# Low halves of the projection weights made on GpSimd in two instructions instead of on VectorE in one

## What is computed

```python
h = _rmsnorm(x, pre_norm[l])
proj = h @ w_in[l]
(a_q, a_k, a_v, sb_q, sb_k, sb_v, f_q, f_k, f_v, f_logit, m_q, gate) = jnp.split(proj, COL_SPLITS, axis=-1)
o_a = _diff_attention(...)      # softmax of two maps, a = p[:, 0] - lam * p[:, 1], then a head norm
o_b = _stick_breaking(...)      # log_sigmoid(z) plus a reversed cumulative sum of log_sigmoid(-z)
o_c = _forgetting_attention(...)  # softmax with a cumulative forget term
o_m = _memory_attention(...)    # 256 memory keys
y = jnp.concatenate([o_a, o_b, o_c, o_m], axis=-1) * jax.nn.silu(gate)
x = x + _rmsnorm(y @ w_out[l], post_norm[l])
```

## Time and profile before

| | us |
|---|---|
| three timed runs | 2762.78, 2762.99, 2768.42 |
| median | 2762.99 |
| profiled execution, its own time | 2765.74 |
| span in its trace | 2763.5 |
| first block | 131 |
| second block | 2249 |
| third block and the change to it | 383.5 |
| PE busy in the second block | 2048.0 |

### The profile page before, as it was taken

The page is one execution under the profiler, slowest core; times in us unless marked ns, Lnnn a source line. Parts: engine busy times, 40 slices in busy tenths (PEclk is TensorE's granted clock), DMA queues, the critical chain, the costliest instruction groups (busy, mean ns, idle before and its releaser), DMA issues. The chain is left out here.

```text
span 2763.5 us, 73142 instructions
## 1 busy us (share of the span) xinstructions
PE 2458.7 (89%) x27422; PEld 1673.8 (61%) x27422; DVE 1814.8 (66%) x5009; ACT 1638.1 (59%) x4453; POOL 1139.3 (41%) x1808
## 2 busy tenths in 40 slices
PE   5589899999899999998989999989999997589998
PEld 4467566666766666666666666666666665334443
DVE  7547798776578887765699877657898765221111
ACT  5336675567667755676677556766775567321121
POOL 6313355456434454564254545642445456200000
PEclk9699999999999999999999999999999999689999
DMA  6235784479858843798598537985884379652331
GB/s 200 75 81 115 130 151 95 66 144 157 160 104 146 145 97 64 141 157 159 94 154 141 103 66 140 156 163 104 147 145 94 60 130 159 162 173 85 113 107 46
DMA packets 934554, 340.56 MB, mean 123 GB/s; under 512 B 766244, under 2 KB 925100, under 8 KB 934188
## 3 DMA queue, kind: packets, MB, share of 16 engines
q1 hardware_dynamic: 933752, 334.83, 61.9%
q0 software_dynamic: 448, 1.05, 0.1%
HBM read 80.83 MB, written 26.84 MB: 39 GB/s over the span
## 5 line engine op out<-in xcount | busy, mean ns | idle before, releaser
L1407 POOL TENSOR_TENSOR rows<-rows 128x512 f16<-128x512 f32 (+3 forms) x864 | 865.9, 1016 | 948.7 <-ACT rows L1365 945.1
L1211 PE MATMUL job<-wt,big 128*128 128x128 f16 x10752 | 680.4, 220 | 46.3 <-DVE gate_s L1497 16.7
L1211 PEld LDWEIGHTS job<-wt,big 128*128 128x128 f16 x10752 | 629.2, 99 | 112.9 <-DVE gate_s L1497 27.4
L1211 PE MATMUL job<-big,wt 128*128 128x512 f16 x2688 | 674.1, 383 | 10.1 <-PEq L672 5.2
L1365 ACT CAST rows<-rows 128x512 f16<-128x512 f32 (+3 forms) x864 | 463.3, 549 | 227.2 <-DVE rows L1489 115.5
L1272 PE MATMUL mixed<-values,rows 128*128 128x64 f16 (+1 forms) x8544 | 446.6, 202 | 107.1 <-DMA rows<-rows 78.3
L1272 PEld LDWEIGHTS mixed<-values,rows 128*128 128x128 f16 x8544 | 393.0, 100 | 235.0 <-DMA rows<-rows 112.2
L1377 ACT ACTIVATE rows<-rows,neg_max 128x512 f32<-128x512 f32 (+3 forms) x704 | 447.7, 638 | 72.7 <-DVE neg_max L1464 70.0
L1456 DVE TENSOR_SCALAR_CACHE_REDUCE rows<-scores 128x512 f32<-128x512 f32 (+3 forms) x704 | 399.6, 587 | 122.3 <-POOL rows L1407 92.9
L1257 PE MATMUL scores<-stack 128*128 128x512 f16 (+3 forms) x1600 | 432.8, 350 | 21.2 <-DVE rows L1456 14.8
L1211 PEld LDWEIGHTS job<-big,wt 128*128 128x128 f16 x2688 | 243.8, 99 | 248.7 <-issue 15.1
(11 more groups left out here) (142 smaller groups left out, 2558.0 us busy)
## 6 DMA issues: line engine op xcount, KB each, us to landing
stack<-planes SPq DMA_DIRECT2D x160, 192.0 KB
ws<-w_in SPq DMA_DIRECT2D x56, 512.0 KB, 4.7
y_halves<-y_out_halves SPq DMA_DIRECT2D x64, 256.0 KB, 2.9
rows<-y_halves SPq DMA_DIRECT2D x16, 1024.0 KB, 8.2
rows<-rows SPq DMA_TRANSPOSE x864, 3.3
rows<-x SPq DMA_DIRECT2D x16, 512.0 KB, 5.1
ws<-w_out SPq DMA_DIRECT2D x16, 512.0 KB, 3.7
stack<-x SPq DMA_DIRECT2D x16, 512.0 KB, 4.8
```

Of the source, the lines that this page charges most:

```text
L1211: last = nc.tensor.matmul(dst, lhs, rhs, start=(k0 == 0 and q == 0), stop=(k1 == KT and q == len(pairs) - 1))
L1407: nc.gpsimd.tensor_tensor(halves_of(tau, 1, w), scored(plan.chunk_at(g, m, k0), 0, w), halves_of(tau, 0, w), ALU.subtract).then_inc(low_po ...
```

## The change

The instruction at L1424 goes from DVE. POOL gets two in its place: a `tensor_scalar` that multiplies the strip by 64 in place in `ws`, and, after a wait for that (semaphore `w_wide`), a `tensor_tensor` that subtracts the high half and writes the low half. In the planner the task `widen` moves from DVE's table to POOL's, behind `lo`, and its length goes from 1.14 to 3.6. All five orders are planned anew with that. No other rank or length differs.

```diff
-    "dve": {"low": 3.02114, "weigh": 3.66090, "lo_dve": 5.58491, "widen": 5.68258, "post": 5.97032,
+    "dve": {"low": 3.02114, "weigh": 3.66090, "lo_dve": 5.58491, "post": 5.97032,
...
-    "pool": {"root": 0.00000, "lo": 1.00000},
+    "pool": {"root": 0.00000, "lo": 1.00000, "widen": 2.00000},
...
-            q["widen"].append((("w_lo", n), ("convert", (n, t, kind)), [("w_hi", n)], 1.14, 0.08))
+            q["widen"].append((("w_lo", n), ("convert", (n, t, kind)), [("w_hi", n)], 3.6, 0.1))
...
+                def convert(c):
+                    n, t, kind = c
+                    hi, lo = wt[:, kind, 0], wt[:, kind, 1]
+                    wide = ws[:, n % 2, :].rearrange("p (k n) -> p k n", k=KT)
+                    pool.wait_ge(w_hi, n + 1)
+                    nc.gpsimd.tensor_scalar(wide, wide, W_SCALE, None, ALU.mult).then_inc(w_wide, 1)
+                    pool.wait_ge(w_wide, n + 1)
+                    nc.gpsimd.tensor_tensor(lo, wide, hi, ALU.subtract).then_inc(w_ready, 1)
...
-                    dve.wait_ge(w_hi, n + 1)
-                    nc.vector.scalar_tensor_tensor(
-                        wt[:, kind, 1], ws[:, n % 2, :].rearrange("p (k n) -> p k n", k=KT), W_SCALE,
-                        wt[:, kind, 0], op0=ALU.mult, op1=ALU.subtract).then_inc(w_ready, 1)
```

More of the change, by code:

```diff
@@ L1022, in build @@
         w_in_sem = [sem(f"w_landed{b}") for b in range(2)]
-        w_hi, w_ready = sem("w_hi"), sem("w_ready")
+        w_hi, w_wide, w_ready = sem("w_hi"), sem("w_wide"), sem("w_ready")
         stacked = [sem(f"stacked{c}") for c in range(NC)]
@@ L1399, in inverse_root @@
                     nc.gpsimd.tensor_tensor(root[:, 3:4], y, rz[:, 0:1], ALU.mult).then_inc(root_step, 1)
+                def convert(c):
[6 more added lines that the diff above has]
+                    nc.gpsimd.tensor_tensor(lo, wide, hi, ALU.subtract).then_inc(w_ready, 1)
                 for op, *args in plan.orders["pool"]:
                     g = args[0]
+                    if op == "convert":
+                        convert(*args)
                     if op == "lo":
@@ L1419, in low @@
                         .then_inc(j_free, 1)
-                def convert(c):
-                    n, t, kind = c
-                    dve.wait_ge(w_hi, n + 1)
-                    nc.vector.scalar_tensor_tensor(
-                        wt[:, kind, 1], ws[:, n % 2, :].rearrange("p (k n) -> p k n", k=KT), W_SCALE,
-                        wt[:, kind, 0], op0=ALU.mult, op1=ALU.subtract).then_inc(w_ready, 1)
                 def stick_chunk(g, n, m, c, w):
@@ L1570, in _ @@
                     g = args[0] if args else None
-                    if op == "convert":
-                        convert(*args)
                     if op == "halves":
```

## The result

The changed kernel takes 2850.2 us (median of 4 runs, 2844.7 to 2857.7) against 2762.9 before. The measured ratio is 1.0325, with a 95% interval of 1.0304 to 1.0346 (the two medians alone give 1.0316, or 87 us). The forecast was 2774 with a range up to 2795. The direction was right and the size was not: +90 us by the ratio instead of +11. In what follows a ratio is turned into us with 2763, so 0.1% is 2.8 us. Rows and busy times are of one profiled execution each, so their differences carry a few us of scatter.

The account below looks back on a forecast made before the run. PE's fixed work plus its idle time was taken as the bound; 2765.7 + 25 - 12 - 8 + 6 = 2777 for the profiled execution, 2774 for the median (2763 + 11). Range 2750 to 2795, the forecast's own 2769 to 2781.

Parts of the forecast that it names:

- The bound: Second block: time is PE's fixed work plus its idle time, 201 us; POOL rises from 48 to some 56%.
- Removed, -12: DVE loses 55 conversions, mostly relieving stick and diff units, so PE waits less for banks: -12 us, bounds 0 and -33.
- Moves on PE, +25: Later strips and moved V and Q jobs give gate banks too little time, so PE idles: +25 us, bounds +10 and +30.
- Mixes later, -8: Stick units of lanes 1 to 3: more work between scores and mix shortens waits for landings: -8 us, bounds 0 and -20.
- Low halves behind the pair, +6: POOL's queue, memory, diff and forget units: low halves delayed, 0.2 us for each of 32 pairs, +6 us, bounds 0 and +60.
- SP and late weights at nothing: SP's strip loads start up to 2.1 us later with transposes behind them; the planned order covers that, cost zero.
- Rival 3: POOL: first instruction as costly as the second, pair 4.7 us, low halves late on an unprepared order; about 2797, chance 0.09.
- Rival 4: Diff units: DVE's two-input instructions blocked at the shared port by POOL pairs; 2774 + 14 = 2788, chance 0.05.
- Rival 1: Stick and diff units: DVE's relief decides, lateness almost gone, bank waits only +14; faster, 2749, chance 0.24.
- Rival 2: PE: bank waits replace waits at the mixes one for one, so no change; 2763, chance 0.22.
- a pair over 4 us: Sign on POOL: if the two new instructions took over 4 us together, POOL's cost would be the wrong term.
- landings above 100: Sign on PE: waits for transposes' landings rising above 100 us would make POOL the cause and not the banks.

Follow-up runs that it names:

- e1: Changed kernel and its orders, both POOL instructions of a conversion on 128 of 1024 columns (pair 0.96 us); ratio 1.0042 to the kernel before, +12 us.
- e4: Kernel before with its old orders, DVE's conversion on 128 of 1024 columns, nothing new on POOL; ratio 0.9963 to the kernel before, -10 us.
- e2: Changed kernel and its orders, first POOL instruction on 512 of 1024 columns, second whole (pair 3.62 us); ratio 1.0168 to the kernel before, +46 us.
- e10: Kernel before's orders, weight factor 1, each conversion moved to POOL as one instruction of 2.13 us; ratio 1.0134 to the kernel before, +37 us.
- e9: Kernel before's orders, all 55 conversions moved from DVE to POOL as the full pair of 4.9 us; ratio 1.0620 to the kernel before, +171 us.
- e3: Changed kernel with the pair's length in the planner 5.0 instead of 3.6, full pair of 4.90 us; ratio 1.0237 to the kernel before, +65 us.
- e11: Orders planned with 5.0 us for the pair, both POOL instructions on 128 of 1024 columns; ratio 1.0072 to the kernel before, +20 us.
- e5: Changed kernel's orders, short pair frees weights early, then four spare pairs on 128 columns that nobody waits for; ratio 1.0358 to the kernel before, +99 us.
- e6: Changed kernel's orders, short pair frees weights early, then 14 memsets of a spare tile, without inputs; ratio 1.0219 to the kernel before, +61 us.
- e7: The change with weight factor 1, one POOL instruction of 2.13 us per conversion, newly planned orders; ratio 1.0156 to the kernel before, +43 us.

## Why the forecast was wrong

**The account.** Orders with a short pair +22 (e1 against e4), relief -10 (e4), the rest of POOL's time +78 (e1 to the changed kernel), together +90. Adding the first two takes it that relief is worth the same on both orders; what e1 shows directly is their sum, 12.

**The bound.** Right. PE's work is fixed in number, POOL never becomes the bound, and what happened went through PE's idle time. What I didn't have: PE's busy time isn't fixed. Between the profiled executions of e1 and the changed kernel the span grows by 87.7 us, of which PE's busy time is 30.8 (2460.0 to 2490.8) and idle time 56.9. Nearly all of the busy time comes in the second half of that step: e2 has 2463.5 us at a mean granted clock of 0.966, as e1 has, and the changed kernel 2490.8 at 0.956. So a third of the loss is slower PE work, and it came when the pair went beyond its planned length. It isn't a fixed surcharge on idle time: e10 is 25 us longer than the kernel before with PE busy for 2 us less (2456.9 against 2458.7).

**Removed, -12.** Right: -10, seen as 8 us less wait for banks.

**Moves on PE, +25.** Right in mechanism, and near in size: +28 of bank waits (e4 to e1), with up to 22 us on the whole together with the landings. The steps of the earlier trace rows stand in the memory unit of lane 1 as walked through:

```profile
758.17 1.51 PE L1211 MATMUL job<-wt,big 128*128 128x128 f16 x24 [0.37 <-DVE gate_s L1501]
...
760.84 1.51 PE L1211 MATMUL job<-wt,big 128*128 128x128 f16 x24 [0.37 <-DVE gate_s L1501]
...
774.14 1.51 PE L1211 MATMUL job<-wt,big 128*128 128x128 f16 x24 [0.70 <-DVE gate_s L1501]
```

Six steps idle 0.37 us and three 0.69 or 0.70.

**Mixes later, -8.** Right in sign, small by half: the landings fall by 16.5 (e4 to e1). The reason isn't shown: in lane 1 they fall from 7.1 to 4.7 us in the stick unit, where I had counted later mixes, and from 3.8 to 1.2 in the diff unit, where I had counted none. With the real pair they are back at 77.0.

**Low halves behind the pair, +6.** This is the step that failed, with 78 us in its place, and it failed in two ways.

The duration: I took 1.1 us for the first instruction, from an affine select of 128 columns at 0.29 us, and allowed 2.35 at most. It took 2.77, outside my bounds, and the pair with 4.90 is beyond the 4.7 too. A TENSOR_SCALAR took 0.53, 0.86, 1.49 and 2.77 us at 128, 256, 512 and 1024 columns, some 2.5 ns a column, while the two-input form takes 1.9 (and 2.35 us in float32 at 1024 columns). The select was another operation in one instance, and that one input can't cost more than two was an assumption that no row bore. The Trainium skill (GPSIMD Engine Reference, section 4.1, Engine selection) calls GpSimd roughly at line rate for one input and about twice slower than VectorE for two; here the one-input form is the dearer, and the measurement decides. The excess over the plan costs 43 us (e2 to the changed kernel).

The price of a microsecond of POOL: even with the length that the plan had, the pair costs 35 us (e1 to e2), where I had 0.2 us for each of 32 pairs. I argued from "Half of POOL's time is free now, so it recovers in two or three chunks", and from a plan that knew of 3.6 us. The premises are true (POOL is busy 48% of the span) and didn't help. The way I read it, the free half is not idle stock: of POOL's 1477 us of idle time in the changed kernel, 766 are waits for ACT's next `hi`. A chunk's way is serial from scores to mix, and what stands in front of its low half is added to it. PE's order is fixed, so it waits at the mix, at the scores (whose buffers come back from POOL by DVE), or at the job whose strip is in that same queue. The runs give the price per us of POOL time: 35 / 146 = 0.24 for the planned part (55 x 2.66), 43 / 70 = 0.61 beyond it (55 x 1.28), and on the old orders 47 / 117 = 0.40 up to 2.13 us and 134 / 152 = 0.88 from there to 4.90 (e10 and e9). On the orders of e3, planned for 5.0, it is 45 / 217 = 0.21 up to 4.90 (e11 and e3). So it grows with length where the orders don't know the length, and not where they do. That buffers and other filler cover a short delay and not a long one would explain it; no run tests that.

**What else stands behind the pair.** The term counted low halves only. POOL also makes the inverse roots of the head norms, for which DVE waits in the diff units. DVE's group behind them, in e1 and then in the changed kernel (busy us, mean ns, idle before it):

```profile
L1557 DVE SCALAR_TENSOR_TENSOR y_f<-o_copy,root,gate_s 128x128 f32<-128x128 f32 x64 | 48.5, 758 | 40.6 <-POOL root L1399 39.9
```

```profile
L1557 DVE SCALAR_TENSOR_TENSOR y_f<-o_copy,root,gate_s 128x128 f32<-128x128 f32 x64 | 50.9, 795 | 58.5 <-POOL root L1399 58.1
```

18 us more of DVE's idle time, by an edge of the graph that the prediction didn't have. How much of it reaches PE wasn't measured; PE's own wait for `y_f` rises only from 4.4 to 5.9 us. The prediction named only the low halves behind the pair.

**SP and late weights at nothing.** Nearly: 9.3 us of PE's wait is for the strip itself, and e5, which has it early, is no faster.

**The rivals.** Rival 3 (slower by POOL) had the mechanism that decided, down to low halves "late on an order that doesn't expect it", and was given 0.09 and 2797. Its price was 25 pairs times the excess of 1.1 us, 28 us where 43 were measured, and it kept the +6 for the planned part, where 35 were. (The sum was also off by itself: 2774 + 28 is 2802, not 2797. And the low end of a pair, 1.0 + 2.2, is 3.2, not 3.1. Neither decides anything.) Rival 4 (the port) shows on DVE: busy time rises by 22 us from e1 to the changed kernel, and the longest combination in the diff units rises from 1.72 to 2.57 us, 1.8 over the median, where the new POOL instructions take 2.13 and 2.77. These are e1 and the changed kernel (ns min/median/max), as the earlier trace rows of before:

```profile
L1493 DVE SCALAR_TENSOR_TENSOR rows<-rows,sc x160: 334/746/1717, 395.5 to 2233.0; 128x512 f32<-128x512 f32 x112, 128x128 f32<-128x128 f32 x16, 128x256 f32<-128x256 f32 x16, 128x384 f32<-128x384 f32 x16
```

```profile
L1493 DVE SCALAR_TENSOR_TENSOR rows<-rows,sc x160: 337/745/2568, 403.8 to 2317.4; 128x512 f32<-128x512 f32 x112, 128x128 f32<-128x128 f32 x16, 128x256 f32<-128x256 f32 x16, 128x384 f32<-128x384 f32 x16
```

This agrees with the rule of the Trainium skill that the prediction weighed (SBUF — State Buffer, "Who interferes with whom"). But e5 loses as much with no such lengthening of DVE (busy 1739.3, longest combination 1.72), so the port isn't what decides. And of the 22 us on DVE 18.5 are there in e2 already (1756.1), so in the step from e2 to the changed kernel, which costs 43, it can hardly have a part. Its share of the 35 before that wasn't measured. Rival 1 is out by e4: relief is worth 10 us. Rival 2, an even trade of bank waits for landings, is half there between e4 and e1 (+28 against -16.5), but the whole rises by 22.

**My own signs.** One pointed right: a pair over 4 us was to mean the cost of POOL, and it took 4.90. The waits at jobs (87.1, over 70), the steps of 0.37 and the landings (77.0, between 70 and 85) also came out as the forecast said, and the forecast was far off all the same. The sign of landings above 100 misled: they stayed at 77.0 and POOL is the cause. The time shows under many names: from e1 to the changed kernel landings +16.5, issue +13.5 (8.5 to 22.0; idle time for which the profile shows no wait), the strip +8.0, values +6.5, the copy of the mix +4.8, scores +4.5, and PE's own slower work +30.8. A single row of waits was no gauge for it, and the starting point of that row had moved by -16.5 with the orders.

## What to carry to other kernels

The idle time of an engine that is a link of a serial chain is mostly waiting for input and not room for work. Here a microsecond put into its queue cost 0.21 to 0.24 us of the whole where the orders were planned for it, besides what those orders cost, and 0.4 to 0.9 where not. It is to be priced by everything that stands behind it there, not by the engine's busy share. Where an operation's duration decides and no row shows that operation, the range goes beyond the dearest form seen, since here one input (float32 in and out) took 1.3 times as long as two (float32 and float16 in, float16 out). And a plan is worth its lengths: with the measured one it took back 25 of 90 us, though no placement on POOL that was tried (whole, in pieces, one step of the two, a part of the strips, old orders or new) was as fast as the conversion on DVE.

## What the runs showed of the hardware

- POOL's one-input `tensor_scalar` in float32 took 0.53 us at 128 columns and 2.77 at 1024, which makes 2.5 ns a column and 0.2 us fixed; the two-input `tensor_tensor` took 0.43 and 2.13, 1.9 ns a column. A `memset` of 128x128 took 0.20 us.
- Two short POOL instructions with a wait between them had 0.07 to 0.08 us of gap (14.4 and 18.4 us over 220 each); the 14 writes in a row of e6 0.05 (41.2 over 770).
- DVE was busy 1759.6 us beside POOL pairs of 2.77 and 2.13 us and 1739.3 beside instructions of 0.54 and 0.43 us with as much POOL time (1379.3 and 1369.8); with a single short pair for each strip it was 1737.6 (e1).
- For the same matmuls PE was busy 2460.0 us at a mean granted clock of 0.966 (e1), 2490.8 at 0.956 (the changed kernel) and 2510.0 at 0.944 (e9). The clock alone doesn't fix it: e7 has 2467.8 at 0.969.
